# From the MLP to the attention: context turned among the last down products, norm sums by panels, the first key products in two halves

## The chip, the core and the metric

The kernel runs on one core of a Trainium2 chip. Its time is the device time of one execution in microseconds (us); three executions of the kernel before took 2696.97, 2700.23 and 2701.65 us, median 2700.23. One more execution was profiled. TensorE (PE) multiplies, VectorE (DVE), ScalarE (ACT) and GpSimd (POOL) do the rest, and SyncE (SP) issues the loads of the weights.

## The reference, cut to what matters

Two transformer blocks run one after the other on 256 tokens of width 2048, all in float32. The place in question is the end of the first block and the start of the second.

```python
x = x + squared_relu_mlp(h, w_mlp_in[l], w_mlp_out[l])      # end of the first block
x = rmsnorm(x, norm_final)
# the second block
sh1, sc1, g1, sh2, sc2, g2 = split(silu(c) @ w_ada + b_ada)  # csh1, csc1 the same from c_ctx
h  = modulate(rms_norm(x, norm_mix_g), sh1, sc1)             # y * (1 + scale) + shift
hc = modulate(rms_norm(ctx, norm_mix_g), csh1, csc1)
y  = neighbourhood_attention(h, hc, w_qkv, ...)              # keys and values of h and hc, queries of h
x  = x + g1 * y
```

Each norm divides a row by the root of its mean square plus 1e-6. So x is normed twice in a row: by `norm_final`, and again for the attention.

## The kernel before, in words

Every product in full precision is three float32r products of split operands: a weight unit (128 rows, 1024 numbers of each) comes by DMA into one of four slots of `raw`, ScalarE copies its rounded part to `whi`, VectorE subtracts to get `wlo` (`split`, lines 611 and 975), and TensorE multiplies hi by hi, hi by lo and lo by hi. The activations stand transposed in `act2` (`ahi`, `alo`), per 128 features k a slot of 512 numbers: 256 tokens in the left half, 256 in the right. The semaphores `hi_done`, `lo_done` and `unit_used` order the units; a slot can be filled again when TensorE has used the unit four before.

The MLP has four groups. In a group 32 up units fill `G[q]` in PSUM and ScalarE and VectorE write the squared ReLU into the right halves of `act2`; then 32 down units (`unit_rows`, line 1554) make four panels of 512 columns in turn in `G[0]` and `G[1]`, and VectorE adds each to x (`add_scaled`, line 1234). Beside that VectorE sums the modulation's columns from `w_ada`, which GpSimd loads (line 510).

After the last panel, in program order: VectorE and ScalarE square one row tile of x each (lines 979 and 615, 2048 numbers a partition), ScalarE forms the root (617, 618), VectorE multiplies by it and by `norm_final` (1301), both square again (`ROW_NORMS` numbers these norms), and both scale into `xs` (984, 827). Meanwhile ScalarE squares and scales the context `ctxr` (822, 829). TensorE then transposes `xs` in eight steps of four 128 by 128 blocks each, and likewise `ctxr` (`turn_rows`, line 1599, turns 3 and 4). For each step ScalarE writes the rounded, modulated value (630), VectorE the unrounded one (997), GpSimd subtracts them into `alo` (540), and TensorE's buffers in PSUM, `X[0]` to `X[3]`, come free with that. x stands in the left halves of `act2`, the context in the right.

The attention has eight turns (`na_turn`) of twelve units: m = 0 to 3 keys for x and context at once (512 tokens wide, line 1911), 4 to 7 queries (1916), 8 to 11 values (1922). The first turn also multiplies a diagonal of the gate g1 by ones to spread it over the partitions (`spread_early`; 1324 builds it, 1929 and 1933 multiply), and each turn sums 32 terms of the later modulation (`ada_tail`, lines 1242 and 1243, 384 wide), whose eight loads GpSimd issues into two buffers (552). A load waits until the one two before it is used up. TensorE adds the sums over the partitions after m = 9 and m = 11 (`ada_sums`, 1808).

The order of work on each engine is the order of the code; nothing reorders it. In the tables of rows, `ps` is PSUM, `act` is `act2`, `arena` the shared scratch area that also holds `xs`, `ctxr`, `nfin` and the loads of `w_ada`.

Of the kernel before, what the change touches and what calls it, by code (L numbers as in the profile page):

```python
# [19 lines left out]
F32 = mybir.dt.float32  # L20
F32R = mybir.dt.float32r
ACT = mybir.ActivationFunctionType
ALU = mybir.AluOpType
# [3 lines left out]
P = 128  # L27
# [94 lines left out]
ROW_NORMS = (0, 2, 3, 4)  # L122
# [36 lines left out]
def program(nc, t, out):  # L159
    ctx = ExitStack()  # L160
    with ctx:
# [13 lines left out]
        ahi, alo = act2[:, 0], act2[:, 1]  # L175
        x = sb("x", [P, RT, D])
# [73 lines left out]
        turned_f = area(8448, 2, 2, S)  # L250
# [11 lines left out]
        psq, rms2 = sb("psq", [P, RT, 4]), sb("rms2", [P, RT])  # L262
        acc3 = sb("acc3", [P, TAIL_W])
# [46 lines left out]
        psq_ok = sem("psq_ok")  # L310
        hid_a, hid_v = sem("hid_a"), sem("hid_v")
# [58 lines left out]
        def _(sp):  # L370
# [94 lines left out]
            for n in range(4):  # L465
                sp.wait_ge(x_done, 4 + n)
# [6 lines left out]
        def _(pool):  # L473
# [55 lines left out]
            for e in range(4, 8):  # L529
                ada_load(ADA_N - 1, e)  # L530
# [12 lines left out]
            turn(3, 0)  # L543
            turn(4, S)

            pool.wait_ge(turned, 8 * 5)
# [19 lines left out]
        def _(act):  # L566
# [232 lines left out]
            with own.loop(0, 4, 4) as g:  # L799
                with own.loop(0, 2, 2) as i:  # L800
                    for j in range(4, 20):
                        split(g * 64 + i * 16 + U_MLP, j)
                        if j % 8 == 3:
# [7 lines left out]
                                           sqr.rearrange("p (c t) -> p c t", t=S), ACT.Copy).then_inc(hid_a, 1)  # L811
                with act.Fori(0, 2) as i:
                    for j in range(4, 20):
                        split(g * 64 + i * 16 + (U_MLP + 32), j)


            act.wait_ge(x_done, 1)
            rms_rows(2, x[:, 0, :], xs[:, 0, :])
            act.wait_ge(ctx_in, 16)
            act.wait_ge(ada_col, ADA_N)  # L820
            for r in range(RT):
                own.done(act.activation(area(4096, D), ctxr[:, r, :], ACT.Square, accum_out=ssum[:, 10 + r:11 + r]))
            own.done(act.activation(rstd[:, 10:12], ssum[:, 10:12], ACT.Ln, scale=1.0 / D, bias=EPS))
            act.activation(rstd[:, 10:12], rstd[:, 10:12], ACT.Exp, scale=-0.5).then_inc(ctx_rs, 1)
            act.wait_ge(x_done, 2)
            rms_rows(3, x[:, 0, :], xs[:, 0, :])
            act.activation(xs[:, 0, :], x[:, 0, :], ACT.Copy, scale=rstd[:, 6:7]).then_inc(xs_ok, 1)
            act.wait_ge(ctx_rs, 1)
            act.activation(ctxr[:, 0, :], ctxr[:, 0, :], ACT.Copy, scale=rstd[:, 10:11]).then_inc(ctx_ok, 1)
            act.wait_ge(coef_ok, 2)  # L830
            turn(3, 0, lambda k: coefs[:, k:k + 1], lambda k: mods[:, k:k + 1])
            turn(4, S, lambda k: coefs[:, 16 + k:17 + k], lambda k: modc[:, k:k + 1])
# [23 lines left out]
            def na_turn(i, first):  # L856
                u0 = i * 12 + U_NA
                for m in range(12):
# [10 lines left out]
                    if m == 6:  # L869
                        inv_rms(i, 0)  # L870
# [25 lines left out]
            act.wait_ge(x_done, 3)  # L896
# [63 lines left out]
        def _(dve):  # L960
# [268 lines left out]
            def add_scaled(n, q, used, done):  # L1229
# [6 lines left out]
                ins.then_inc(done, 1)  # L1236
# [26 lines left out]
            def mlp_half(g, up, cx):  # L1263
# [756 lines left out]
```

## Time and profile before

| | us |
|---|---|
| median of three runs | 2700.23 |
| the profiled execution | 2695.33 |
| its span, first to last instruction | 2693.1 |
| TensorE busy | 2569.5 |
| VectorE, ScalarE, GpSimd busy | 1743.4, 1152.9, 183.2 |

The profile is of one execution of 2695.33 us; the 2.2 us beside its span lie around the first and last instruction. Busy shares are over the whole span. A matmul's busy time overlaps its successor's, so a unit's length is read from the starts or from the merged pieces of the chain of waits, not from the mean of one. The granted clock is a share of 2.4 GHz: 0.5 is the level of 1.2 GHz. Times of single rows count from the span's start.

### The profile page before, as it was taken

What the parts mean: (1) busy time and instruction counts of PE and PEld (TensorE: products, weight loads), DVE (VectorE), ACT (ScalarE), POOL (GpSimd) and SP (SyncE); (2) the same over time, 40 slices, a digit from 0 to 9 for tenths busy, and PEclk for the clock granted to TensorE, in tenths of its full rate; (3) what the DMA queues carried; (4) which work ended last, traced back from release to release, by engine and by line L of the source; (5) the groups of instructions that cost most, each with busy time, mean ns of one, the idle gap of its engine ahead of it and who ended that gap; (6) DMA issues with size and microseconds to landing.
All of it is one profiled execution on the core that took longest, in us unless ns stands there. A gap on an engine that the chain in (4) does not pass through costs nothing.

```text
span 2693.1 us, 42214 instructions
## 1 busy us (share of the span) xinstructions
PE 2569.5 (95%) x15397; PEld 2272.8 (84%) x15397; DVE 1743.4 (65%) x2194; ACT 1152.9 (43%) x1421; POOL 183.2 (7%) x213
## 2 busy tenths in 40 slices
PE   4999988999999999996999999998889999999999
PEld 4989877998988989985888888886678888888887
DVE  4555455778877876667666666665556665666576
ACT  3444344543443543445233333333455534554453
POOL 2100004000000000003000000000010000000000
PEclk8999999999999999997999999998989999999999
DMA  6743369778777877772666665652546656656555
GB/s 159 247 124 98 117 192 265 267 233 275 237 247 244 259 240 248 251 238 90 194 194 193 193 186 181 191 174 82 184 125 187 187 191 183 187 187 202 179 181 173
DMA packets 277976, 523.87 MB, mean 195 GB/s; under 512 B 30697, under 2 KB 100897, under 8 KB 277089
## 3 DMA queue, kind: packets, MB, share of 16 engines
q1 hardware_dynamic: 251616, 403.66, 47.3%
q0 software_dynamic: 25536, 118.29, 14.6%
q8 instruction: 81, 1.33, 0.2%
q10 hardware_dynamic: 704, 0.29, 0.0%
q14 instruction: 39, 0.31, 0.0%
HBM read 511.68 MB, written 10.49 MB: 194 GB/s over the span
## 4 chain that ended last, share of the span: by engine, by line
PE 47%; DVE 3%; ACT 1%; issue 1%; POOL 1%; DMA 0%; ACTq 0%; POOLq 0%; DVEq 0%; SPq 0%
PE ps L1554 12%; PE ps L1573 11%; PE ps L1911 6%; PE ps L1576 6%; PE ps L1922 5%; PE ps L1916 3%; PE ps L1879 1%; PE ps L1858 1%; POOL act L540 1%; PE ps L1887 1%; DVE acc L1243 1%; PE ps L1867 1%; ACT whi L611 0%; DVE wlo L975 0%; PE ps L1808 0%
## 5 line engine op out<-in xcount | busy, mean ns | idle before, releaser
L975 DVE TENSOR_TENSOR wlo<-raw,whi 128x1024 fp32r<-128x1024 f32 (+2 forms) x776 | 939.1, 1218 | 589.6 <-ACT whi L611 569.5
L611 ACT ACTIVATE whi<-raw 128x1024 fp32r<-128x1024 f32 (+2 forms) x776 | 803.3, 1040 | 993.4 <-PE ps L1554 407.7
L1554 PE MATMUL ps<-whi,act 128*128 128x512 f32 (+2 forms) x2608 | 794.2, 386 | 18.4 <-DVE wlo L975 16.2
L1554 PEld LDWEIGHTS ps<-whi,act 128*128 128x128 f32 x2608 | 485.9, 190 | 113.0 <-DVE wlo L975 15.1
L1546 PE MATMUL ps<-act,whi 128*128 128x256 f32 (+2 forms) x2880 | 529.9, 286 | 12.9 <-DVE wlo L975 10.8
L1554 PE MATMUL ps<-wlo,act 128*128 128x512 f32 (+2 forms) x1304 | 501.0, 384 | 0.0
L1546 PEld LDWEIGHTS ps<-act,whi 128*128 128x128 f32 (+1 forms) x2880 | 453.2, 192 | 15.0 <-issue 11.3
L1546 PE MATMUL ps<-act,wlo 128*128 128x256 f32 (+2 forms) x1440 | 410.6, 285 | 0.0
L1573 PE MATMUL ps<-act,whi 128*128 128x512 f32 x1376 | 378.4, 396 | 5.9 <-POOL act L540 4.6
L1554 PEld LDWEIGHTS ps<-wlo,act 128*128 128x128 f32 x1304 | 247.1, 190 | 45.8
L1243 DVE SCALAR_TENSOR_TENSOR arena<-arena,cond 128x768 f32<-128x768 f32 (+1 forms) x330 | 278.7, 867 | 4.6 <-DMA arena<-in_w_ada 1.8
L1546 PEld LDWEIGHTS ps<-act,wlo 128*128 128x128 f32 (+1 forms) x1440 | 276.5, 192 | 1.3 <-issue 1.3
L1573 PEld LDWEIGHTS ps<-act,whi 128*128 128x128 f32 x1376 | 235.5, 189 | 37.8 <-issue 5.0
L1576 PEld LDWEIGHTS ps<-act,wlo 128*128 128x128 f32 x1376 | 212.6, 189 | 30.1
L1576 PE MATMUL ps<-act,wlo 128*128 128x256 f32 x1376 | 220.7, 281 | 0.0
L1922 PE MATMUL ps<-whi,act 128*128 128x256 f32 x1024 | 192.1, 290 | 0.0
L1922 PEld LDWEIGHTS ps<-whi,act 128*128 128x128 f32 x1024 | 160.4, 192 | 7.7 <-issue 7.7
L1911 PE MATMUL ps<-act,whi 128*128 128x512 f32 x512 | 164.4, 402 | 0.0
L1922 PE MATMUL ps<-wlo,act 128*128 128x256 f32 x512 | 144.8, 283 | 0.0
L1911 PEld LDWEIGHTS ps<-act,whi 128*128 128x128 f32 x512 | 95.4, 190 | 22.0 <-issue 3.9
L1911 PE MATMUL ps<-act,wlo 128*128 128x512 f32 x256 | 100.6, 393 | 0.0
L1916 PE MATMUL ps<-act,whi 128*128 128x256 f32 x512 | 98.4, 293 | 0.0
(254 smaller groups left out, 1938.6 us busy)
## 6 DMA issues: line engine op xcount, KB each, us to landing
arena<-in_w_ada POOLq DMA_DIRECT2D x128, 768.0 KB, 5.6
raw<-in_ffn_w_up SPq DMA_DIRECT2D x160, 512.0 KB, 4.4
raw<-in_w_mlp_in SPq DMA_DIRECT2D x128, 512.0 KB, 5.1
raw<-in_w_mlp_out SPq DMA_DIRECT2D x128, 512.0 KB, 4.8
raw<-in_na_w_qkv SPq DMA_DIRECT2D x96, 512.0 KB, 4.7
raw<-in_ffn_w_down SPq DMA_DIRECT2D x84, 512.0 KB, 4.5
raw<-in_w_in SPq DMA_DIRECT2D x64, 384.0 KB, 3.4
raw<-in_w_in SPq DMA_DIRECT2D x32, 512.0 KB, 4.6
```

Source lines behind the costliest of these rows:

```text
L540: pool.tensor_tensor(alo[:, k, off:off + S], turned_f[:, at % 2], ahi[:, k, off:off + S].bitcast(F32), ALU.subtract).then_inc(a_lo, 2)
L611: act.activation(a, b, ACT.Copy).then_inc(hi_done, 1)
L975: dve.tensor_tensor(a, b, c, ALU.subtract).then_inc(lo_done, 1)
L1243: return dve.scalar_tensor_tensor(out=acc, in0=piece, scalar=sc, in1=acc, op0=ALU.mult, op1=ALU.add)
L1546: ins = pe.matmul(o, a, b, start=start and i == 0, stop=last and i == 2, skip_group_check=True)
L1554: ins = pe.matmul(o, a, b, start=start and i == 0, stop=last and i == 2, skip_group_check=True)
L1573: pe.matmul(Z[q][:, c, :].rearrange("p (h t) -> p h t", h=2), kn(whi, j)[:, kk, P * c:P * c + P], act2[:, :, k, 0:S], start=k == 0, stop=k ...
L1576: ins = pe.matmul(Z[q][:, c, 0:S], kn(wlo, j)[:, kk, P * c:P * c + P], ahi[:, k, 0:S], start=False, stop=k == KC - 1, skip_group_check=True)
L1858: pe.matmul(X[1], qT[:, hh, P * qb:P * qb + P], kT[:, hh, :], start=True, stop=True).then_inc(n_s, 1)
L1911: ins = pe.matmul(G[0][:, c, :], a, b, start=st and y == 0, stop=sp_ and y == 2)
L1916: ins = pe.matmul(X[0][:, S * c:S * c + S], a, b, start=st and y == 0 and c == 0, stop=sp_ and y == 2, skip_group_check=True)
L1922: ins = pe.matmul(Gf[1][:, S * r:S * r + S], a, b, start=st and y == 0 and r % 2 == 0, stop=sp_ and y == 2, skip_group_check=True)
```

## The change

The rows of the context are squared, scaled, transposed and modulated before and during the last group: its squares and its root stand between the third group and the fourth; its eight turn steps stand behind every second down unit of the last group's first two panels (`ctx_step`). The two norms of x are formed together: for each panel of 512 columns, as soon as it is complete, ScalarE squares x and x times `norm_final` (`final_squares`, `final_product`), so that after the last panel one panel's squares are left; the scale for `xs` comes from both sums at once, and x itself gets its first norm later (`residual_rows`, in the first turn's m = 0). x now stands in the right halves of `act2`, where the hidden values were, and the context in the left half of the next slot. The first turn's keys are made for the context first and for x after (`first_keys`), x's turn steps between. In the other seven turns the last of the sixteen k of the key units is multiplied as two pieces of 256 instead of one of 512. The gate's spreading moves behind m = 4 and 6, the first turn's `ada_tail` slots to m = 5 to 11.

```diff
+FIRST_TAIL = {5: (0,), 6: (1,), 7: (2,), 8: (3, 4, 5), 9: (6, 7, 8), 10: (9, 10), 11: (11,)}
-ROW_NORMS = (0, 2, 3, 4)
+ROW_NORMS = (0, 4)
...
+        def own_rows(h, c, t0, n):
+            return act2[:, h, c, S + t0:S + t0 + n]
+        def ctx_rows(h, c, t0, n):
+            at = (512 * c + 512) % (512 * KC)
+            return both[:, h, at + t0:at + t0 + n]
...
+            for e, steps in ((4, (0, 1)), (5, (2, 3)), (6, (4, 5)), (7, (6, 7))):
+                ada_load(ADA_N - 1, e)
+                for at in steps:
+                    turn_lo(3, at)
+            for at in range(8):
+                turn_lo(4, at)
-            pool.wait_ge(turned, 8 * 5)
+            pool.wait_ge(x2_ok, 1)
...
+            mlp_up(3)
+            def final_squares(n):
+                act.wait_ge(drained[n % 2], D_MLP[n % 2] - 1 + n // 2)
+                for r in range(RT):
+                    own.done(act.activation(junk_a, x[:, r, cs], ACT.Square, accum_out=fsq[:, r, n:n + 1]))
+                act.wait_ge(y_ok, n + 1)
+                for r in range(RT):
+                    own.done(act.activation(junk_a, xs[:, r, cs], ACT.Square, accum_out=fsq[:, 2 + r, n:n + 1]))
...
+            for j in range(4, 35):
+                split(U_MLP + 3 * 64 + 32, j)
+                if j % 2 == 1 and j < 20:
+                    turn_step(3, (j - 5) // 2)
+                if j % 8 == 5 and j > 8:
+                    final_squares(j // 8 - 1)
...
+            act.wait_ge(fvar_ok, 1)
+            own.done(act.activation(frms[:, 1, :], frms[:, 0, :], ACT.Ln))
+            act.activation(frms[:, 1, :], frms[:, 1, :], ACT.Exp, scale=-0.5).then_inc(frms_ok, 1)
+            act.wait_ge(frms_ok, 1)
+            scale_piece(0, xs, xs, frms[:, 1, 0:1])
+            scale_piece(1, xs, xs, frms[:, 1, 0:1])
+            split(U_NA, 3)
+            turn_step(4, 0)
...
+            own.done(dve.tensor_reduce(fsum[:, :], fsq[:, :, :], AXX, ALU.add))
+            own.done(dve.tensor_scalar(frms[:, 0, :], fsum[:, 0:2], EPS / D, EPS * EPS, ALU.mult, ALU.add))
+            dve.scalar_tensor_tensor(out=frms[:, 0, :], in0=fsum[:, 2:4], scalar=1.0 / D, in1=frms[:, 0, :],
+                                     op0=ALU.mult, op1=ALU.add).then_inc(fvar_ok, 1)
...
+            def residual_rows():
+                dve.wait_ge(r1_ok, 1)
+                for r in range(RT):
+                    own.mark(dve.scalar_tensor_tensor(out=x[:, r, :], in0=x[:, r, :], scalar=frms[:, 2, r:r + 1], in1=nfin,
+                                                      op0=ALU.mult, op1=ALU.mult))
+                own.wait()
+                dve.sem_inc(x2_ok, 1)
...
+            def ctx_step(at):
+                if at >= 2:
+                    pe.wait_ge(a_lo, TURN_AT[3] + 2 * at - 2)
...
+                            if last and i == 0 and j % 2 == 1:
+                                ctx_step(4 * q + j // 2)
...
+            def own_steps(steps):
+                for at in steps:
+                    pe.wait_ge(xs_a, at // 2 + 1)
+                    pe.wait_ge(xs_v, at // 2 + 1)
...
+            def first_keys():
+                pe.wait_ge(a_lo, TURN_AT[4])
+                for m in range(4):
+                    pe.wait_ge(lo_done, U_NA + m + 1)
+                    half_keys(m, *w(m), ctx_rows, S, True)
+                    if m:
+                        own_steps(range(2 * m - 2, 2 * m))
+                for m in range(4):
+                    pe.wait_ge(a_lo, TURN_AT[4] + 4 * m + 4)
+                    half_keys(m, *w(m), own_rows, 0, False).then_inc(unit_used, 1)
+                    if m == 0:
+                        own_steps(range(6, 8))
...
-                    if first and m == 0:
+                    if first and m == 4:
                         pe.wait_ge(gb_ok, 1)
```

TensorE from the last down product to the first key products. Before, 16 steps of four transposes stand in one piece between the down products (line 1554) and the keys (1911).

```order
L1554 MATMUL ps<-whi,act2 128x512 x2
L1554 MATMUL ps<-wlo,act2 128x512
L1841 REGISTER_ALU
L1841 COMPARE_AND_BRANCH
L1599 MATMUL ps<-cst,arena 128x128 x64
L1911 MATMUL ps<-act2,whi 128x512 x2
L1911 MATMUL ps<-act2,wlo 128x512
```

After, the context's transposes (line 1996 of the changed kernel) stand among the down products (1726), four at a time.

```order
L1726 MATMUL ps<-whi,act2 128x512 x2
L1726 MATMUL ps<-wlo,act2 128x512
L1996 MATMUL ps<-cst,arena 128x128 x4
L1726 MATMUL ps<-whi,act2 128x512 x2
L1726 MATMUL ps<-wlo,act2 128x512
```

And x's (2046) stand, eight at a time, between half-wide key products (2056).

```order
L2056 MATMUL ps<-act2,whi 128x256 x2
L2056 MATMUL ps<-act2,wlo 128x256
L2046 MATMUL ps<-cst,arena 128x128 x8
L2056 MATMUL ps<-act2,whi 128x256 x2
L2056 MATMUL ps<-act2,wlo 128x256
```

The 64 transposes are divided into twelve pieces, eight in the down products and four in the keys, and the keys are twice as many and half as wide.

VectorE from the last panel's addition (1234 before, 1332 after) to the gate's diagonal (1324 before, 1492 after). Before:

```order
L1234 SCALAR_TENSOR_TENSOR x<-ps,rms,x 128x512 x2
L1284 COPY mods<-ps 128x6
L151 REGISTER_ALU
L151 COMPARE_AND_BRANCH
L979 ISA arena,stat<-x 128x2048
L979 ISA stat 128x1
L1301 SCALAR_TENSOR_TENSOR x<-x,stat,arena 128x2048 x2
L979 ISA arena,stat<-x 128x2048
```

After, from the root's last term to the diagonal (1463 scales `xs`, 1425 is the turn step, 1481 the residual's norm, 1073 a split):

```order
L1457 SCALAR_TENSOR_TENSOR frms<-fsum,frms 128x2
L1463 TENSOR_SCALAR arena<-arena,frms 128x512 x2
L1073 TENSOR_TENSOR wlo<-raw,whi 128x1024
L1425 TENSOR_SCALAR arena<-ps,coefs,mods 128x256 x2
L1463 TENSOR_SCALAR arena<-arena,frms 128x512
L1425 TENSOR_SCALAR arena<-ps,coefs,mods 128x256 x2
L1463 TENSOR_SCALAR arena<-arena,frms 128x512
L1425 TENSOR_SCALAR arena<-ps,coefs,mods 128x256 x12
L1481 SCALAR_TENSOR_TENSOR x<-x,frms,arena 128x2048 x2
L1073 TENSOR_TENSOR wlo<-raw,whi 128x1024
L1490 TENSOR_TENSOR mods<-mods,cols 128x16
L1492 TENSOR_SCALAR arena<-cst,mods 128x128 x16
```

The long product with `norm_final` has moved from ahead of the transposes to behind them, and it stands ahead of the split of the first query unit and of the diagonal.

VectorE at the end of the first turn (m = 9 to 11). Before:

```order
L1243 SCALAR_TENSOR_TENSOR acc<-arena,cond,acc 128x384 x4
L975 TENSOR_TENSOR wlo<-raw,whi 128x1024
L1243 SCALAR_TENSOR_TENSOR acc<-arena,cond,acc 128x384 x4
L1368 SCALAR_TENSOR_TENSOR arena<-ps,cols,arena 128x512
L1388 COPY mods<-ps 128x3
L975 TENSOR_TENSOR wlo<-raw,whi 128x1024
L1243 SCALAR_TENSOR_TENSOR acc<-arena,cond,acc 128x384 x4
```

After:

```order
L1347 SCALAR_TENSOR_TENSOR arena<-arena,cond 128x384 x2
L1346 TENSOR_SCALAR acc<-arena,cond 128x384
L1347 SCALAR_TENSOR_TENSOR acc<-arena,cond,acc 128x384 x3
L1073 TENSOR_TENSOR wlo<-raw,whi 128x1024
L1347 SCALAR_TENSOR_TENSOR acc<-arena,cond,acc 128x384 x8
L1536 SCALAR_TENSOR_TENSOR arena<-ps,cols,arena 128x512
L1556 COPY mods<-ps 128x3
L1073 TENSOR_TENSOR wlo<-raw,whi 128x1024
L1347 SCALAR_TENSOR_TENSOR acc<-arena,cond,acc 128x384 x4
```

Six terms stand at m = 9 now and eight at m = 10, where four and four stood; none is left at m = 0 to 4.

## Rows read from the trace of the kernel before

**Rows 1.** The page of before: busy time of the two busiest engines.
```profile
PE 2569.5 (95%) x15397; PEld 2272.8 (84%) x15397; DVE 1743.4 (65%) x2194; ACT 1152.9 (43%) x1421; POOL 183.2 (7%) x213
```

**Rows 2.** Stretches after the down products: length; busy PE, PEld, DVE, ACT, POOL; clock; DMA; GB/s.
```profile
1230.20:1266.60 36.40, 16.61 (x64) 11.84 (x64) 28.28 (x44) 28.80 (x47) 15.76 (x13) 0.53 0.08 26
1266.60:1277.10 10.50, 10.11 (x33) 6.98 (x33) 6.95 (x21) 2.31 (x4) 5.84 (x6) 0.85 0.36 107
1277.10:1293.40 16.30, 16.30 (x74) 13.48 (x74) 10.63 (x15) 2.12 (x2) 2.51 (x4) 1.00 0.74 238
1293.40:1333.10 39.70, 39.39 (x310) 37.26 (x309) 25.84 (x34) 14.24 (x18) 3.49 (x6) 1.00 0.67 209
1333.10:1402.70 69.60, 69.30 (x460) 61.74 (x460) 45.29 (x75) 23.14 (x35) 6.55 (x10) 1.00 0.61 188
```

**Rows 3.** Timeline of TensorE around the seam: start, length, work, idle before.
```profile
1229.77 0.39 PE L1554 MATMUL ps<-wlo,act 128*128 128x512 f32 x1
1246.61 3.67 PE L1599 MATMUL ps<-cst,arena 128*128 128x128 f32 x16 [16.45 <-ACT arena L827]
1251.95 2.35 PE L1599 MATMUL ps<-cst,arena 128*128 128x128 f32 x8 [1.67 <-POOL act L540]
...
1266.67 1.20 PE L1911 MATMUL ps<-act,whi 128*128 128x512 f32 x2
```

**Rows 4.** Timeline of VectorE in the same stretch.
```profile
1232.43 1.40 DVE L1234 SCALAR_TENSOR_TENSOR x<-ps,rms,x 128x512 f32<-128x512 f32 x2
...
1236.88 4.61 DVE L1301 SCALAR_TENSOR_TENSOR x<-x,stat,arena 128x2048 f32<-128x2048 f32 x2 [0.57 <-ACT stat L618]
...
1249.46 1.90 DVE L997 TENSOR_SCALAR arena<-ps,coefs,mods 128x256 f32<-128x256 f32 x4 [2.43 <-ACT act L630]
...
1269.42 4.70 DVE L1324 TENSOR_SCALAR arena<-cst,mods 128x128 f32<-128x128 f32 x16
...
1287.96 0.62 DVE L1243 SCALAR_TENSOR_TENSOR arena<-arena,cond 128x384 f32<-128x384 f32 x1 [1.76 <-DMA arena<-in_w_ada]
```

**Rows 5.** Timeline of ScalarE, same stretch.
```profile
1236.41 0.20 ACT L617 ACTIVATE stat<-stat 128x2 f32<-128x2 f32 x1 [0.50 <-DVE stat L979]
...
1248.35 3.73 ACT L630 ACTIVATE act<-ps,mods,coefs 128x256 fp32r<-128x256 f32 x8
```

**Rows 6.** Timeline of GpSimd, same stretch.
```profile
1250.64 20.32 POOL L540 TENSOR_TENSOR act<-arena,act 128x512 fp32r<-128x512 f32 x16 [69.06 <-DVE arena L997]
...
1281.46 0.75 POOL L552 DMA_DIRECT2D arena<-in_w_ada  x1 [8.04 <-DVE arena L1243]
```

**Rows 7.** Chain of waits, in order of time: attention units at full clock.
```profile
1277.07 16.33 PE ps L1911 x72
...
1300.02 2.87 PE ps L1916 x24
...
1319.54 5.85 PE ps L1922 x48
```

**Rows 8.** TensorE earlier: transposes at full clock.
```profile
428.54 1.04 PE L1599 MATMUL ps<-cst,x 128*128 128x128 f32 x8
```

**Rows 9.** ScalarE earlier: one square of 512 with its sum.
```profile
478.00 0.63 ACT L786 ACTIVATE arena<-x 128x512 f32<-128x512 f32 x1
478.54 0.19 ACT L786 ACTIVATION_READ_ACCUMULATOR arena<-x 128x1 f32 x1
```

**Rows 10.** VectorE at the boundary of turns 0 and 1.
```profile
1329.67 2.57 DVE L1243 SCALAR_TENSOR_TENSOR acc<-arena,cond,acc 128x384 f32<-128x384 f32 x4
1333.31 0.16 DVE L1388 COPY mods<-ps 128x3 f32 x1 [1.06 <-PE ps L1808]
```

**Rows 11.** Loads of the modulation's columns (line 552).
```profile
DMA to landing us min/median/max: 4.9/5.3/7.5
```

**Rows 12.** VectorE's splits with and without GpSimd beside them.
```profile
442.58 7.75 DVE L975 TENSOR_TENSOR wlo<-raw,whi 128x1024 fp32r<-128x1024 f32 x4
...
459.61 1.23 DVE L975 TENSOR_TENSOR wlo<-raw,whi 128x1024 fp32r<-128x1024 f32 x1 [1.19 <-ACT whi L611]
```

More of the change, by code:

```diff
@@ L798, in _, with mlp_up @@
             act.sem_inc(psq_ok, 1)
-            with own.loop(0, 4, 4) as g:
+            def mlp_up(g):
                 with own.loop(0, 2, 2) as i:
@@ L814, in _ @@
                         split(g * 64 + i * 16 + (U_MLP + 32), j)
-            act.wait_ge(x_done, 1)
-            rms_rows(2, x[:, 0, :], xs[:, 0, :])
             act.wait_ge(ctx_in, 16)
-            act.wait_ge(ada_col, ADA_N)
             for r in range(RT):
-                own.done(act.activation(area(4096, D), ctxr[:, r, :], ACT.Square, accum_out=ssum[:, 10 + r:11 + r]))
+                for half in range(2):
+                    own.done(act.activation(area(3072, 1024), ctxr[:, r, 1024 * half:1024 * half + 1024], ACT.Square,
+                                            accum_out=fsq[:, r, half:half + 1]))
@@ L835, in attend_a @@
+            for at in range(3, 8):
+                turn_step(4, at)
             def attend_a(i, m):
@@ L869, in na_turn @@
                     if m == 6:
+                        if first:
+                            act.wait_ge(x2_ok, 1)
                         inv_rms(i, 0)
@@ L1267, in mlp_half @@
                     for j in range(4, 20):
-                        split(u0, j)
+                        end = last and i == 1 and j == 19
+                        if not end:
+                            split(u0, j)
                         slot = 16 * i + j - 4
@@ L1317, in _ @@
-            turn(3, 0, lambda k: coefs[:, k:k + 1], lambda k: mods[:, k:k + 1])
-            turn(4, S, lambda k: coefs[:, 16 + k:17 + k], lambda k: modc[:, k:k + 1])
+            dve.wait_ge(nf_in, 16)
+            mlp_half(3, False, False, True)
+            cs3 = slice(1536, D)
+            for r in range(RT):
+                ins = dve.tensor_tensor(xs[:, r, cs3], x[:, r, cs3], nfin[:, cs3], ALU.mult)
+                if r == 0:
+                    ins.then_inc(y_ok, 1)
+                else:
+                    own.done(ins)
@@ L1890, in na_turn @@
                 u0 = i * 12 + U_NA
-                for m in range(12):
+                if first:
+                    first_keys()
+                for m in range(4 if first else 0, 12):
                     part = m // 4
@@ L1930, in na_turn @@
                         ins.then_inc(gb_mm, 1)
-                    if first and m == 5:
+                    if first and m == 6:
                         pe.wait_ge(gb_rd, 1)
```

230 lines of the change are left out of this document (176 added, 54 removed).

## The prediction

> **What bounds the kernel now.** First the page: TensorE is busy for 2569.5 of 2693.1 us [rows 1], so a change pays only where TensorE stands or runs slowly. Then the busy times by stretch [rows 2]: the reader is to see that the 36.4 us after the last down product hold only 16.6 us of TensorE at 0.53 of its clock, and that the next stretches are full at 1.00. Then TensorE's timeline [rows 3]: the last down product ends at 1230.2 (E below), 16.45 us are empty, and from 1246.6 on 64 transposes run in bursts that GpSimd releases, until the first key product at 1266.7. The timelines of the other three say why. Ahead of the transposes stands a chain on VectorE and ScalarE in which every link handles 2048 columns, the longest 4.61 us [rows 4]. In the transposes GpSimd works without a break, 20.32 us for 16 steps, 1.27 each [rows 6]. The first group of keys then waits once more, for the gate's diagonal, which ends at 1274.1 [rows 4].
>
> I measure from E to the start of turn 1 at 1333.1: 102.9 us before. Behind it the eight turns are periodic, 69.6 us at 69.3 busy [rows 2], and the change touches them in one place only.
>
> **What the change costs outside the seam.** Eight context steps of four transposes go into the last down units. Eight transposes at full clock took 1.04 us, start to end [rows 8], some 0.13 each with the overlap off; 0.55 a step, 4.4 us in all, wholly on TensorE's path. The bounds are 0.5 and 1.27 a step (GpSimd's pace, if a buffer is not free), 4 to 10; I take 4.4, since a buffer has two steps, some 12 us, to come free. A down unit is twelve 512-wide products. 72 of them in the keys took 16.33 us [rows 7], so 0.227 each and 2.72 a unit. In two units and a step, 6.0 us, VectorE has two splits (1.23 each [rows 12]), one 768-wide term (at most two of the 384-wide at 0.62 [rows 4], 1.24) and a turn step (0.95 [rows 4]), 4.65 in sum; ScalarE two copies of about 1.1, a step of 0.94 [rows 5] and, at three places, four squares of 0.73 [rows 9]. Both fit, and the splits run three units ahead, which covers the 2.6 us of addition and product at a panel's end. So nothing more falls on the path. The context's squares, root and scaling on ScalarE at the start of the fourth group take four squares of 1024 (an estimate from the 512-wide at 0.73: 1.2), two small operations of 0.2 with hand-overs (0.8) and one copy of 2048 (four of 512-wide at 0.5: 2.0), about 7.6 us with the split's 1.1 ahead 8.7, against four up units (2.88 each, as 24 products of 256 took 2.87 [rows 7]): just covered with a split and its subtraction behind it, 0 to 2 us, I take 0. The last k of the keys as 256-wide pieces costs 12 times 0.12 instead of 6 times 0.227 in each of seven turns, 0.5 us together.
>
> **The seam after, from E.** VectorE adds the last panel by rows, 1.4 us [rows 4]; ScalarE squares behind it. VectorE forms the last product and a square over 512 columns, 1.25 and 0.7; three small operations 0.9, two on ScalarE 0.5 [rows 5], one scaled piece 0.6. Sum with hand-overs: xs's first piece stands at E+5.5. TensorE meanwhile does the context half: 96 products of 256, 2.88 a unit. It wants its first x step after two of them, at E+5.8. This margin of 0.3 is thin, and the last links are estimates from rows of other widths; bounds for the wait are 0 and 3, I take 0. The x steps then run on ScalarE in E+7 to E+20.3 (each 0.94 to 1.02, with a split of 1.06, two scalings and the second root between), one behind on VectorE until E+21.3, and on GpSimd until E+22.6. TensorE needs them only unit by unit in the second half; its own work is 8 times 2.88 plus 32 transposes at 0.137, so the keys end at E+27.4 against E+63.2 before.
>
> From there VectorE sets the pace. Behind its last turn step at E+21.3 stand in order: the two long products, 4.6 [rows 4]; a split, 1.2; the gate's diagonal, 0.2 and 4.6 [rows 4]. That is E+32.1. The query unit ends at E+30.3, so TensorE waits 1.8 us and its three gate products end at E+34.7. VectorE goes on with four splits, 4.6, and the gate's copy, 1.7, and starts its 32 terms only at E+38.4, where before nine were already done when the keys ended. A load takes, from the term that frees its buffer to its use, 6.5 us: 1281.46 [rows 6] to 1287.96 [rows 4]; from issue to landing 4.9 to 7.5, median 5.3 [rows 11]. Walking through m = 5 to 11 with terms at 0.62, splits at 1.2 and norms at 0.75: the third load is wanted at E+47.0 and there at E+48.4; the fifth at E+57.2, there at E+60.0; the seventh at E+66.2, there at E+68.9. The last four terms, 2.57 as at 1329.67 [rows 10], end at E+75.9. TensorE's own work from the keys' end (the wait of 1.8, the gate 3.4, four units of 2.87, four of 5.75 [rows 7], the norm and column sums 3.2) ends at E+70.3, so it stands for 5.6 us before the last column sums. Turn 1 starts at E+76.8, 26.1 earlier than before. Before, it waited there too, but for a fraction: 1329.67 plus 2.57 is 1332.2, and turn 1's first work follows at 1333.1. After so long a stand the first products run at 1.2 GHz; at 1266.7 that stretch of 10.5 us showed 0.85 of the clock [rows 2], a loss of 1.5, and I take 1.3.
>
> Sum: -26.1 + 4.4 + 0.5 + 1.3 = -19.9 us. The profiled execution, 2695.3, becomes 2675.4. It lay 4.9 below the median of the three runs, so against this median I predict 2680.3.
>
> **A rule that speaks against it.** With GpSimd's work beside them, four splits of VectorE took 7.75 us, 1.94 each; without it one took 1.23 [rows 12]. In the change GpSimd's last two x steps fall beside the two long products at E+21.3. By a delay of this size they end some 1.4 us later, and the keys about as much; VectorE's list behind it shifts by 0.7 at most, and the time with it. The Trainium skill (SBUF — State Buffer, engine ports and the shared port pair) says that VectorE's instructions with two SBUF inputs and GpSimd's exclude one another for the whole instruction. By that rule, an estimate, GpSimd could stand for both long products, the last keys would end 2.7 us later, and about 1 us of it would reach turn 1. The trace agrees that the two slow each other, and cannot show the order of the two here.
>
> **The rivals.**
> Dense end: the terms are not late, because loads land sooner or VectorE's list is shorter than I count. For it: TensorE alone is done at E+70.3, and in the turns of before loads stopped VectorE for 1.76 us once [rows 4]. Against: VectorE begins the terms some 10 us after the keys. The stand of 5.6 and the clock's 1.3 fall away: -26.8, 2673.4.
>
> Broken first keys: the norm's root comes late and TensorE stands inside the keys, so that its clock falls while narrow products and short transposes alternate. For it: margin 0.3, and in bursts of transposes the clock stayed at 0.5 for 20 us [rows 2, 3]. Against: products stand between, and at 428.5 transposes among products went at full pace [rows 8]. If half the keys run at 1.2 GHz, they take 12 to 14 more, of which the stand of 5.6 absorbs a part: -10 to -14, about 2688. If all do, 25 more: -1, 2699, no change.
>
> Slower: the last group's down products lose the pace. VectorE's turn step waits for ScalarE's, ScalarE's for the transposes, and GpSimd's subtraction, now beside splits and terms with two SBUF inputs, adds 0.7 to each of three operations in a pair of units [rows 12]: 4.65 becomes 6.75 against 6.0. That alone costs 6 over eight pairs. It decides once short stands pull the clock down: at 1.2 GHz the 16 units take 43 more, of which 14 more suffice to undo the gain: 6 + 43 - 20 is 29 slower at the full price, 2729. The splits' three units in hand speak against.
>
> **How the numbers follow.** Forecast 0.47; dense end 0.20; broken keys in part 0.22, in full 0.03; slower 0.05; 0.03 for a gain beyond the dense end. For the forecast alone the range is 2675 to 2686 (VectorE's list by 3 us either way, runs by 2). The whole range takes in the dense end and the broken keys in part: 2668 to 2692. What a measurement tells from no change is about 0.2%, 5.4 us, so faster has the forecast, the dense end and all partial cases: 0.92; same 0.03; slower 0.05.
>
> **What would show it.** In the profile after: the context transposes among down units that otherwise keep 2.72; the first x transposes some 6 us after the last down product, TensorE above 95% busy at clock 1.00 until the gate; keys done near E+27; a wait of about 2 us for the gate's diagonal; loads of `w_ada` as releasers of VectorE at m = 7, 9 and 10; a wait of 5 to 6 us before line 1808's successor, released by VectorE's terms; turn 1 at E+77. It is wrong if the clock falls inside the keys, if the down units of the last group lengthen, or if turn 1 starts before E+72 or after E+82.

## The result, and the profile after

| | before | after |
|---|---|---|
| median of five runs, us | 2698.93 | 2686.70 |
| lowest and highest | 2696.54 to 2701.65 | 2682.38 to 2691.88 |
| profiled execution, and its span | 2695.33, 2693.1 | 2682.38, 2680.7 |

The ratio of the times is 0.995, 95% interval 0.9934 to 0.9966: 13.5 us faster, between 9.2 and 17.8 (the medians themselves differ by 12.2). Predicted were 2680.3, a range of 2668 to 2692, and 19.9 us of gain. So the sign and the whole range held; the gain came out smaller, and the forecast's own narrower range, 2675 to 2686, was missed by 0.7.

The page of the changed kernel: TensorE is busy for as long as before [rows 1], in a shorter span.

```profile
PE 2569.4 (96%) x15535; PEld 2281.1 (85%) x15535; DVE 1747.9 (65%) x2205; ACT 1159.0 (43%) x1454; POOL 197.9 (7%) x221
```

Busy times by stretch, columns as in [rows 2]. E, the end of the last down product, is now 1239.5.

```profile
1239.50:1266.90 27.40, 26.68 (x224) 26.30 (x222) 21.24 (x33) 17.05 (x34) 12.45 (x8) 1.00 0.11 37
1266.90:1280.00 13.10, 12.18 (x82) 10.15 (x81) 12.36 (x27) 4.09 (x4) 1.51 (x2) 1.00 0.83 277
1280.00:1298.50 18.50, 17.43 (x133) 16.03 (x131) 14.21 (x20) 6.96 (x9) 3.02 (x5) 1.00 0.87 275
1298.50:1317.30 18.80, 13.96 (x106) 13.28 (x105) 12.70 (x20) 4.15 (x5) 3.52 (x5) 0.92 0.72 235
1317.30:1387.90 70.60, 70.36 (x459) 62.55 (x458) 45.21 (x75) 21.30 (x32) 5.79 (x8) 0.97 0.59 185
```

Where 36.4 us held 16.6 of TensorE at a clock of 0.53, 27.4 us now hold 26.7 at 1.00: the keys are done in them as well. The last two lines carry what spoils it: the end of turn 0 is short of work (13.96 of 18.80), and turn 1 runs at 0.97 and takes 70.6 where it took 69.6.

TensorE's timeline, from the first context step on (columns as in [rows 3]; products left out). Lines of the changed kernel: 1996 context steps, 2046 x steps, 2056 first keys, 2152 queries, 2166 gate, 1980 column sums.

```profile
1152.49 0.66 PE L1996 MATMUL ps<-cst,arena 128*128 128x128 f32 x4 [1.50 <-DVE arena L1441]
...
1158.49 0.60 PE L1996 MATMUL ps<-cst,arena 128*128 128x128 f32 x4
...
1245.23 1.06 PE L2046 MATMUL ps<-cst,arena 128*128 128x128 f32 x8
...
1249.01 1.04 PE L2046 MATMUL ps<-cst,arena 128*128 128x128 f32 x8
...
1264.00 0.50 PE L2056 MATMUL ps<-act,whi 128*128 128x256 f32 x2 [0.69 <-POOL act L569]
...
1267.62 0.47 PE L2152 MATMUL ps<-act,whi 128*128 128x256 f32 x2 [0.48 <-DVE wlo L1073]
...
1271.16 2.84 PE L2166 MATMUL ps<-arena,cst 128*128 128x512 f32 x6 [0.44 <-DVEq L1494]
...
1297.78 0.80 PE L1980 MATMUL ps<-cst,arena 128*128 128x1 f32 x6 [1.07 <-DVE arena L1347]
...
1315.88 1.44 PE L1980 MATMUL ps<-cst,acc 128*128 128x1 f32 x6 [4.84 <-DVE acc L1347]
1317.18 1.20 PE L2147 MATMUL ps<-act,whi 128*128 128x512 f32 x2
```

These are all waits above 0.3 us between the first context step and turn 1. The 16.45 us of [rows 3] and GpSimd's bursts are gone; what stands instead is 4.84 us before the last column sums, released by VectorE's terms, and the two products behind it take 1.20 us where at full clock they take 0.62 to 0.71. The busy times there, the clock at its lower level of 1.2 GHz:

```profile
1316.00:1321.00 5.00, 5.00 (x15) 4.23 (x16) 1.35 (x2) 0.00 (x0) 0.75 (x1) 0.50 0.95 293
```

VectorE in the same stretch (1481 products for x, 1492 the gate's diagonal, 1346 and 1347 the terms):

```profile
1244.33 0.88 DVE L1463 TENSOR_SCALAR arena<-arena,frms 128x512 f32<-128x512 f32 x2 [0.58 <-ACT frms L915]
...
1260.03 6.07 DVE L1481 SCALAR_TENSOR_TENSOR x<-x,frms,arena 128x2048 f32<-128x2048 f32 x2
...
1267.59 3.45 DVE L1492 TENSOR_SCALAR arena<-cst,mods 128x128 f32<-128x128 f32 x16
...
1277.41 0.41 DVE L1346 TENSOR_SCALAR arena<-arena,cond 128x384 f32<-128x384 f32 x1
...
1287.97 0.62 DVE L1347 SCALAR_TENSOR_TENSOR arena<-arena,cond 128x384 f32<-128x384 f32 x1 [1.75 <-DMA arena<-in_w_ada]
...
1300.44 0.42 DVE L1346 TENSOR_SCALAR acc<-arena,cond 128x384 f32<-128x384 f32 x1 [2.81 <-DMA arena<-in_w_ada]
...
1308.77 2.58 DVE L1347 SCALAR_TENSOR_TENSOR acc<-arena,cond,acc 128x384 f32<-128x384 f32 x4 [2.19 <-DMA arena<-in_w_ada]
...
1313.25 2.57 DVE L1347 SCALAR_TENSOR_TENSOR acc<-arena,cond,acc 128x384 f32<-128x384 f32 x4
```

The first term starts 10 us after the keys are done, loads are then waited for, and the last four terms end at 1315.8, where TensorE had run out of work at 1311.0.

Four rows of column sums mark the program in every version: A, at the end of the last group's up half; B, 4.3 us before E; C, at the end of turn 0; D, at the end of the last turn. All the versions run below, with the differences between the starts of these rows, from one profile each, in us. Each ratio is to executions of before taken beside that version (medians 2698.9 to 2700.9):

| kernel | median, us | ratio to before | A to B | B to C | C to D |
|---|---|---|---|---|---|
| before | 2698.93 | 1 | 88.56 | 106.38 | 487.37 |
| after | 2686.70 | 0.9950 (0.9934 to 0.9966) | 94.04 | 80.67 | 490.22 |
| tail_early | 2676.40 | 0.9921 (0.9906 to 0.9935) | 94.03 | 75.39 | 487.81 |
| terms_cut | 2674.32 | 0.9914 (0.9896 to 0.9932) | 94.03 | 75.58 | 487.79 |
| steps_first | 2693.77 | 0.9976 (0.9967 to 0.9986) | 94.03 | 90.64 | 490.27 |
| squares_late | 2689.64 | 0.9958 (0.9944 to 0.9972) | 94.05 | 88.21 | 490.08 |
| ctx_late | 2708.13 | 1.0027 (1.0016 to 1.0038) | 88.56 | 109.77 | 489.89 |
| both_mended | 2673.68 | 0.9897 (0.9883 to 0.9911) | 92.31 | 75.69 | 487.84 |
| rows_wait | 2675.26 | 0.9899 (0.9869 to 0.9929) | 92.31 | 76.02 | 487.82 |

From before to after the three stretches give +5.5, -25.7 and +2.9, together -17.4. The two spans differ by 12.4. The missing 5.0 lie where both kernels run the same instructions: 0.9 up to the first group's column sums at 577, 2.9 from there to the end of the third group, 1.2 behind the last turn. Where the times of two versions are compared below, the difference of their ratios is taken, times 2700.

### The profile page after: what moved, and what is told of

It is laid out like the page before. It is cut to its first block, busy times and chain, and to the rows that moved or that the text cites. A ratio compares the mean times of both kernels' runs of the same rounds, so it can differ in the third digit from the quotient of the medians.

```text
span 2680.7 us, 42529 instructions
## 1 busy us (share of the span) xinstructions
PE 2569.4 (96%) x15535; PEld 2281.1 (85%) x15535; DVE 1747.9 (65%) x2205; ACT 1159.0 (43%) x1454; POOL 197.9 (7%) x221
## 4 chain that ended last, share of the span: by engine, by line
PE 86%; DVE 6%; DMA 3%; ACT 2%; issue 1%; SPq 1%; ACTq 0%; POOL 0%; POOLq 0%; DVEq 0%
PE ps L1726 30%; PE ps L1718 18%; PE ps L1745 12%; PE ps L1748 6%; PE ps L2147 5%; PE ps L2159 5%; PE ps L2152 3%; DMA raw<-in_w_in 1%; PE ps L2106 1%; SPq L434 1%; PE ps L2085 1%; DVE wlo L1073 1%; DVE acc L1347 1%; PE ps L1980 1%; PE ps L2114 1%
## 5 line engine op out<-in xcount | busy, mean ns | idle before, releaser
L1745 PE MATMUL ps<-act,whi 128*128 128x512 f32 x1376 | 379.3, 396 | 6.3 <-POOL act L555 4.9
L1726 PEld LDWEIGHTS ps<-wlo,act 128*128 128x128 f32 x1304 | 247.5, 190 | 45.7
L1745 PEld LDWEIGHTS ps<-act,whi 128*128 128x128 f32 x1376 | 236.1, 190 | 38.4 <-issue 5.3
L2147 PE MATMUL ps<-act,whi 128*128 128x512 f32 x420 | 135.7, 405 | 0.0
L935 ACT ACTIVATE arena<-arena,nst 128x512 f32<-128x512 f32 x32 | 23.2, 724 | 175.2 <-DVE nst L1520 175.2
L2159 PEld LDWEIGHTS ps<-wlo,act 128*128 128x128 f32 x512 | 98.0, 191 | 0.0
```

The source lines that it names most:

```text
L1726: ins = pe.matmul(o, a, b, start=start and i == 0, stop=last and i == 2, skip_group_check=True)
L1745: pe.matmul(Z[q][:, c, :].rearrange("p (h t) -> p h t", h=2), kn(whi, j)[:, kk, P * c:P * c + P], act2[:, :, k, 0:S], start=k == 0, stop=k ...
L2147: ins = pe.matmul(G[0][:, c, :], a, b, start=st and y == 0, stop=False, skip_group_check=True)
L2159: ins = pe.matmul(Gf[1][:, S * r:S * r + S], a, b, start=st and y == 0 and r % 2 == 0, stop=sp_ and y == 2, skip_group_check=True)
```

## The experiments

**Are VectorE's late terms what stops TensorE? (tail_early)** The terms of the first turn are handed out by loads instead of by slots, as many as have landed: eight already at m = 5, and the second sum from m = 9.

```diff
-FIRST_TAIL = {5: (0,), 6: (1,), 7: (2,), 8: (3, 4, 5), 9: (6, 7, 8), 10: (9, 10), 11: (11,)}
+FIRST_TAIL = {5: (0, 8), 7: (8, 12), 8: (12, 16), 9: (16, 24), 10: (24, 28), 11: (28, 32)}
...
-                        for slot in FIRST_TAIL.get(m, ()):
-                            ada_tail(i, slot)
+                        if m in FIRST_TAIL:
+                            ada_tail(i, None, range(*FIRST_TAIL[m]))
```

> The changed kernel with the 32 terms of the first turn's modulation dealt out otherwise: eight at m = 5, none at 6, four at 7 and 8, eight at 9, four at 10 and 11, so that both buffers are free for the next loads by about 1282.5 on the changed kernel's time axis (1286.2 there). Theory A (the stand before turn 1 is the alternation of loads and terms on VectorE): the last term ends at about 1311 instead of 1315.8, TensorE's two waits for terms (4.8 and 1.1 us) shrink to 1 or less and turn 1 starts at full clock; 6 to 8 us faster than the changed kernel's 2686.7, so about 2679. Rival B (the loads themselves cannot come sooner, since weights share the queues): within 2 us of 2686.7.

TensorE's timeline at the end of turn 0, and the busy times from there to the end of turn 1:

```profile
1311.64 0.83 PE L1980 MATMUL ps<-cst,acc 128*128 128x1 f32 x6 [0.85 <-DVE acc L1347]
```

```profile
1298.00:1311.60 13.60, 12.79 (x102) 12.11 (x101) 11.34 (x18) 3.82 (x5) 2.25 (x3) 1.00 0.86 271
1311.60:1381.30 69.70, 69.36 (x464) 62.02 (x464) 45.23 (x75) 22.64 (x34) 6.56 (x9) 1.00 0.62 195
```

The wait falls from 4.84 to 0.85 and the one of 1.07 goes; B to C is 5.3 shorter, C to D 2.4, together 7.7; the ratios differ by 7.8 us, as expected. So the stand cost its own length and 2.4 of clock behind it, where I had put 1.3.

**The same with the terms taken away (terms_cut).** Twenty-two of the first turn's 32 terms are left out, so that part of the modulation isn't summed.

```diff
+                    if cut and k and k % 4 != 3:
+                        continue
                     ins = ada_term(s, k, ada2[:, q % 2, k % 4, :], (acc2, acc3[:, :])[s], 0, k == 0)
```

> The changed kernel without 22 of the 32 terms of the first turn's modulation (only the first of each sum and the last of each load are left); the loads all stay. Theory A: VectorE is free for the loads' pace, TensorE does not stand before turn 1: 6 to 8 us faster than 2686.7. Rival B (only the loads' pace counts): the last load lands as late as before, gain 0 to 2 us. Rival C (the time of the changed kernel is lost outside the seam, in the clock's dips during the MLP): the stand goes away in the trace, and the median moves by less than its spread of 5 us.

```profile
1313.20 0.83 PE L1982 MATMUL ps<-cst,acc 128*128 128x1 f32 x6 [1.05 <-DVE acc L1347]
```

VectorE's last term there:

```profile
1312.53 0.62 DVE L1347 SCALAR_TENSOR_TENSOR acc<-arena,cond,acc 128x384 f32<-128x384 f32 x1 [1.94 <-DMA arena<-in_w_ada]
```

It is 9.7 us faster than after, a little more than the 6 to 8 expected; the rival that the time was lost outside the seam is out. With a third of the work B to C is 75.6, no less than in tail_early. The 1 us that is left waits for the last load here. In tail_early no load is waited for at that place: the last four terms follow a split at once, from 1309.0 to 1311.6. So either way of removing the lateness leaves TensorE about 1 us.

**Is it the interleaving that keeps the clock up? (steps_first)** All x steps stand ahead of the keys.

```diff
                 pe.wait_ge(a_lo, TURN_AT[4])
+                own_steps(range(8))
                 for m in range(4):
                     pe.wait_ge(lo_done, U_NA + m + 1)
                     half_keys(m, *w(m), ctx_rows, S, True)
-                    if m:
-                        own_steps(range(2 * m - 2, 2 * m))
```

> The changed kernel with all eight x turn steps ahead of the first key products, context half then x half unbroken. Theory A (VectorE's list sets the start of turn 1, and TensorE has slack of 6 us in the first turn): the keys end some 11 us later (about E+39), the steps 3 to 5 us sooner, and the whole is 3 to 6 us slower than 2686.7, with the clock's fall in it. Rival D (the gain lies in the context products under x's norm): 11 to 14 us slower, which gives back the whole gain.

TensorE's timeline, and the busy times from E on:

```profile
1246.04 3.65 PE L2046 MATMUL ps<-cst,arena 128*128 128x128 f32 x16 [5.77 <-DVE arena L1463]
1251.09 0.66 PE L2046 MATMUL ps<-cst,arena 128*128 128x128 f32 x4 [1.40 <-POOL act L569]
1252.50 0.65 PE L2046 MATMUL ps<-cst,arena 128*128 128x128 f32 x4 [0.75 <-POOL act L569]
1253.82 2.34 PE L2046 MATMUL ps<-cst,arena 128*128 128x128 f32 x8 [0.67 <-POOL act L569]
```

```profile
1239.00:1266.60 27.60, 18.90 (x112) 17.12 (x111) 20.43 (x32) 13.87 (x31) 12.35 (x8) 0.75 0.14 42
```

TensorE stands for 8.6 us and the stretch runs at 0.75 of the clock instead of 1.00. The keys end at E+40.6. B to C grows by 10.0, the time by 7.0: more than the 3 to 6 that I expected, less than the rival's 11 to 14. The terms' stand shrinks to 3.71, so only a part of the loss is absorbed there. The interleaving of context keys and x steps is thus worth 7 to 10 us of the gain.

**Are the squares by panels worth anything? (squares_late)** All squares of ScalarE wait until its last weight split.

```diff
-                if j % 8 == 5 and j > 8:
-                    final_squares(j // 8 - 1)
+            for n in range(3):
+                final_squares(n)
             cs3 = slice(1536, D)
```

> The changed kernel with the squares of the first three panels (twelve squares of 512 on ScalarE) behind the last split instead of among the down units. Theory A: the norm's root comes 12 x 0.76 = 9.1 us later less what ScalarE finds free before the last panel (about 2), so xs's first piece is at E+11 to 13 instead of E+5.8, TensorE stands 5 to 7 us inside the first keys, and everything behind on VectorE moves with it: 7 to 11 us slower than 2686.7, with the clock's fall. Rival D: the norm sums are hidden either way, 0 to 2.

```profile
1257.96 1.94 PE L2046 MATMUL ps<-cst,arena 128*128 128x128 f32 x8 [4.71 <-DVE arena L1463]
```

TensorE now waits for the scale of `xs`, 4.71 us, and the transposes behind it take 1.94 where they took 1.06: half clock. B to C grows by 7.5, as theory A has it. The time grows only by 2.2, where 7 to 11 were expected, and the two intervals overlap. The profiled execution is the slowest of the ten (2698.1, median 2689.6), and the granted clock over the whole execution was 0.981 in five of them (2683.0 to 2690.5 us) but 0.976 to 0.978 in the other five, this one included (2685.8 to 2698.1). The profile shows the mechanism in one execution; whether every execution pays for it, and what it costs in time, is not settled by these runs.

**The context's steps behind the last down product (ctx_late).** The steps are moved whole: TensorE's, ScalarE's, VectorE's and GpSimd's, which issues its four loads ahead of them. Besides, the context's unrounded values go to another place in the scratch area, and so do the square's discarded values on VectorE, and VectorE's third product no longer waits for GpSimd's steps.

```diff
-                            if last and i == 0 and j % 2 == 1:
-                                ctx_step(4 * q + j // 2)
...
             mlp_turn(3, None, last=True)
+            for at in range(8):
+                ctx_step(at)
```

> The changed kernel with the context's eight turn steps behind the last down product (on ScalarE and VectorE behind the first two scaled pieces of x) instead of among the down units. Theory A: the down units lose 5.5 us (eight steps of 0.5 and the wait of 1.5), but the steps take 8 x 1.27 at GpSimd's pace from E+6 on, and the context's keys and all of VectorE's list come behind them: turn 1 starts 10 to 12 us later after E; net 5 to 8 us slower than 2686.7, with a fall of the clock in the stand before. Rival D (the steps were not worth moving, since they cost TensorE full time among the down units): 0 to 3 us slower or faster.

TensorE's and GpSimd's timelines (1994 the context steps there, 565 the subtractions for them):

```profile
1249.56 1.11 PE L1994 MATMUL ps<-cst,arena 128*128 128x128 f32 x4 [9.92 <-POOL act L565]
1250.92 1.12 PE L1994 MATMUL ps<-cst,arena 128*128 128x128 f32 x4 [0.25 <-POOL act L565]
1254.36 1.12 PE L1994 MATMUL ps<-cst,arena 128*128 128x128 f32 x4 [2.33 <-POOL act L565]
1255.73 1.12 PE L1994 MATMUL ps<-cst,arena 128*128 128x128 f32 x4 [0.26 <-POOL act L565]
```

```profile
1252.90 2.77 POOL L565 TENSOR_TENSOR act<-arena,act 128x256 fp32r<-128x256 f32 x4 [2.04 <-DVE arena L1418]
1257.71 2.78 POOL L565 TENSOR_TENSOR act<-arena,act 128x256 fp32r<-128x256 f32 x4 [2.03 <-DVE arena L1418]
```

```profile
1250.00:1270.00 20.00, 10.85 (x45) 8.48 (x44) 5.97 (x12) 6.12 (x12) 9.21 (x14) 0.50 0.01 3
```

It is slower than before by 7.3 us (4.3 to 10.3), and 21 slower than after, where I expected 5 to 8. I had counted GpSimd's pace, 1.27 a step. The rows show another limit: with two buffers a pair of steps comes round every 4.8 us (1249.56, 1254.36, and 1252.90 to 1257.71), GpSimd stands for 2.04 of it, and TensorE's clock is at 0.50 throughout. In [rows 6], with four buffers, GpSimd never stood. A to B is 88.56, the value of before, so the steps alone make the 5.5 us of the down half; and having them there saves far more than it costs.

**The best of both (both_mended).** The wait of 1.50 before the first context step is VectorE's scaling of the context's second row tile (line 1441), which stands in its program behind the last group's whole up half. Here tail_early is kept and the scaling stands ahead of that half.

```diff
+            dve.wait_ge(ctx_rs, 3)
+            dve.tensor_scalar(ctxr[:, 1, :], ctxr[:, 1, :], rstd[:, 11:12], None, ALU.mult).then_inc(ctx_ok, 1)
             mlp_half(3, True, False)
-            dve.wait_ge(ctx_rs, 3)
-            dve.tensor_scalar(ctxr[:, 1, :], ctxr[:, 1, :], rstd[:, 11:12], None, ALU.mult).then_inc(ctx_ok, 1)
```

> tail_early, and besides the scaling of the context's second row tile on VectorE moved from behind the fourth group's up half to ahead of it, where VectorE stands 3.5 us for ScalarE. Theory A: the wait of 1.5 us ahead of the first context step, which every trace of the changed kernel has, goes away and nothing takes its place; 1 to 2 us faster than tail_early's 2676.4, 10 to 13 faster than the changed kernel. Rival: the wait is replaced by one for the first up units of the group, no gain over tail_early.

TensorE's timeline at the first context step, no wait ahead of it:

```profile
1148.97 0.60 PE L1996 MATMUL ps<-cst,arena 128*128 128x128 f32 x4
```

A to B is 92.31 instead of 94.03, 1.7 less. At 2673.68 this has the lowest median: a ratio of 0.9897 to before, 27.8 us, twice the change's own gain. Against tail_early I expected 1 to 2 us. The ratios differ by 6.5, but their intervals overlap; the trace shows 1.7 of it.

**Do the long products and GpSimd exclude each other? (rows_wait)** both_mended, but VectorE starts its two products for x only when GpSimd has done its last subtraction.

```diff
                 dve.wait_ge(r1_ok, 1)
+                dve.wait_ge(a_lo, OT_AT)
                 for r in range(RT):
```

> both_mended with one wait more: VectorE's two long products for the residual wait until GpSimd's last x step is done. Theory G (the two engines exclude each other: each product of 2048 columns holds GpSimd's next piece back and the other way round): GpSimd's last two pieces take 2.5 us together instead of 4.6, the two products 4.6 instead of 6.1; TensorE's wait of 0.70 us in the keys goes, the products end within 0.6 us of before, and the time stays within 1 us. Rival H (the products are slow by themselves, through their scalar's source): the products still take 6.1, all behind moves by 2.4 us and the time by 1 to 2.5.

VectorE's, GpSimd's and TensorE's timelines:

```profile
1264.29 4.61 DVE L1482 SCALAR_TENSOR_TENSOR x<-x,frms,arena 128x2048 f32<-128x2048 f32 x2 [1.91 <-POOL act L569]
```

```profile
1261.64 2.54 POOL L569 TENSOR_TENSOR act<-arena,act 128x512 fp32r<-128x512 f32 x2 [1.22 <-DVE arena L1425]
```

```profile
1270.43 0.47 PE L2153 MATMUL ps<-act,whi 128*128 128x256 f32 x2 [1.98 <-DVE wlo L1073]
```

Apart from one another the two take 4.61 and 2.54; together, in after, 6.07 and 4.57, and the same in both_mended. So the products aren't slow by themselves (rival H). The wait for GpSimd (0.69) goes, one of 1.98 for VectorE's split comes, B to C is 0.3 longer, and the time is the same within its interval.

**Both kernels unchanged, once more each (before_again, after_again).**

> The kernel before, unchanged, for a second trace. Theory E (how often the clock falls near the column sums of the first three groups, untouched by the change, is chance): the spans from the first column sums (576.5) to those at the end of the third group (1041.1, so 464.6 in the first trace) comes out anywhere from 464 to 468. Rival F (the changed kernel is slower there for a reason in its code): again 464.6, within 0.5.

> The changed kernel, unchanged, for a second trace. Theory E: the same span, 467.5 in its first trace, varies by 1.5 us or more. Rival F: again 467.5 within 0.5. Both expect the last down product to turn 1's column sums at 76.4 within 0.5, since no load and no clock decides there.

They took 2698.30 and 2686.81. A to B, B to C and C to D came again: 88.55, 106.45 and 487.43 for before, 94.03, 80.85 and 490.55 for after, so -17.0 us in place of -17.4. The last down product to turn 1's column sums took 76.6, within the 0.5 expected, though loads have a part in it: VectorE's terms wait for them.

The stretch from the first group's column sums to the end of the third group, the same instructions in all versions, took 464.6 us in the profile of before, 467.5 in that of after, but 467.6 and 467.7 in the repeats, and 465.0 in those of tail_early and both_mended. The repeat of after alone came as rival F has it; the repeat of before, and the two versions with after's code there, rule F out. So the 2.9 us between the first two profiles are not the change's. Busy times of before and of after where such a loss lies, the first row a part of the second:

```profile
952.40:955.80 3.40, 3.40 (x18) 3.40 (x18) 0.00 (x0) 0.00 (x0) 0.00 (x0) 0.51 0.65 227
952.00:977.00 25.00, 25.00 (x118) 21.51 (x118) 15.96 (x19) 11.39 (x11) 0.71 (x1) 0.93 0.56 186
```

```profile
652.00:677.00 25.00, 25.00 (x121) 21.16 (x121) 15.60 (x16) 8.41 (x8) 1.43 (x2) 0.93 0.76 247
```

TensorE is busy all the time, and the clock falls to its lower level of 1.2 GHz for a few microseconds. Such a fall follows some of the short bursts of column sums, one burst in each half of a group, 2 to 4 us behind the burst's start. Of the six bursts from 577 to 1050 it followed three in before (falls at 580, 952 and 1044), all six in after, and four in each repeat. From the first burst to the second every profile took 91.4 us with one fall and 89.9 without, so one costs 1.5. Up to the end of the third group after has five of them and before two, so three more, 4.6 us by this price. A shorter wait of TensorE near 860, 0.51 us in after where before has 0.89 and 1.17, gives 1.5 of it back, which leaves about the 2.9. Why one burst is followed by a fall and the next isn't stays open.

## Why the prediction was right, and where it was off

**The seam.** Predicted from E: first x transposes at +5.8, measured +5.7; keys done +27.4, measured +27.7; gate's products start at +32.1 after a wait of 1.8, measured +31.7 after 0.44, with 0.69 and 0.48 of short waits ahead that I hadn't; first term +38.4, measured +37.9; last term ends +75.9, measured +76.3; turn 1's first key product +76.8, measured +77.7, against 102.9 before. So -25.2 where I had -26.1. 0.6 of the 0.9 between the two are the column sums ahead of turn 1, which ran at half clock: from their start to turn 1's first key product it is 1.30, in terms_cut 0.69. The margin before the first x transposes is as thin as it was counted, 0.3: TensorE starts on them at 1245.23, the first scaled piece was done at 1244.8 on VectorE and at 1245.0 on ScalarE. The profile of squares_late shows the price of missing it.

**Two errors in VectorE's list that cancel.** The two products for x took 6.07, not 4.6; the gate's diagonal 3.45, not 4.6. That 1.5 too little and 1.2 too much cancel is luck. Both come from GpSimd. One line of each kernel, for its single instructions (minimum, median, maximum in ns; first and last start):

```profile
L1324 DVE TENSOR_SCALAR arena<-cst,mods x16: 268/278/1336, 1269.4 to 1273.8; 128x128 f32<-128x128 f32 x16
```

```profile
L1492 DVE TENSOR_SCALAR arena<-cst,mods x16: 269/282/595, 1267.6 to 1270.8; 128x128 f32<-128x128 f32 x16
L1481 DVE SCALAR_TENSOR_TENSOR x<-x,frms,arena x2: 2783/3072/3361, 1260.0 to 1262.7; 128x2048 f32<-128x2048 f32 x2
L569 POOL TENSOR_TENSOR act<-arena,act x4: 1288/1291/3321, 1255.6 to 1260.6; 128x512 fp32r<-128x512 f32 x4
```

Of before's sixteen pieces of the diagonal one, the second, took 1336 ns: it ended at 1271.05, just behind GpSimd's last subtraction, which ends at 1270.96 [rows 6]. The 4.6 that I carried over from [rows 4] contained this wait. That GpSimd caused it is read from these times and from its absence in after; no run tests it. For the products, in after, the order is plain: the first product ended at 1262.82; GpSimd's last subtraction, begun at 1260.63, ended at 1263.95, 1.1 behind it; the second product, begun at 1262.74, ended at 1266.10, 2.2 behind that. Alone they take 1.3 and 2.3. So that subtraction took 3321 ns instead of 1290, and each product was held back by one subtraction at most. In the prediction such a delay put the end of the last keys 1.4 us later by [rows 12], 2.7 by the page's rule with GpSimd standing for both products. GpSimd stood for one; of its 2.0 us 0.69 reached TensorE, and the keys ended 0.3 behind the forecast. The Trainium skill (SBUF — State Buffer, who interferes with whom) says that a VectorE instruction with two inputs in SBUF contends with a GpSimd instruction that reads SBUF, and that whoever issues first holds the shared ports for the whole instruction. The trace agrees, and rows_wait shows both durations without the other.

**The stand and the clock.** Predicted 5.6 for the wait and 1.3 for the clock; measured 4.84 and 1.07 in two places, 5.9 together, and 2.4. The clock's term was mis-sized: I took it from a stretch of 10.5 us at 0.85 [rows 2], but here the column sums ahead of turn 1 and its first products ran at half clock, 0.50 from 1316 to 1321. tail_early and terms_cut remove both at once and bring turn 1 back to 69.7 us.

**The down half.** Predicted 4.4, measured 5.5. The eight steps cost 0.47 each, their spacing of 5.9 less two units of 2.72, and 3.75 in all (A to B of both_mended less before's), where I took 0.55. The rest, 1.7, is the wait of 1.50 and what hangs on it, for VectorE's scaling of the context. I had priced the context's norm at 0 to 2 on ScalarE, took 0, and never asked for the half of it that stands on VectorE behind 32 splits. That is the step that failed: of a moved chain I followed one engine only. both_mended shows 1.7 us for it.

**The turns.** The last k in two pieces: predicted 0.5, measured 0.4 to 0.5 (C to D 487.8 in the versions without the stand, 487.4 before).

**The sum.** The traced terms give -17.4 where I had -19.9; 1.1 of the difference is the down half, 0.9 the seam, the rest, 0.5, the clock behind turn 1's start. The measured gain is 13.5, with 17.4 still inside its interval (9.2 to 17.8). Between the two lie stretches that the change doesn't touch; in the repeats these differ by up to 3 us from one execution to the next, through falls of the clock. Whether all of these 4 us are chance is not shown: over the other versions the traced gain exceeds the measured one by up to 3.8 (tail_early) and falls short by up to 1.3 (both_mended, squares_late).

**The rivals.** Dense end: it didn't come, but tail_early is that case made on purpose, 7.7 us better in the trace where the rival was priced 6.9 better. Broken keys in part: by the number alone, 13.5, it would fit this rival's price of 10 to 14, but the clock stayed at 1.00 in the keys; steps_first and squares_late show what it costs when the pace breaks, 10.0 and 7.5 in the profile, where the rival was priced 6 to 10 worse than the forecast. Down products losing pace: no wait above 0.3 in them but the first.

## What to carry to other kernels

When work is pulled forward out of a gap, price what stood in the gap's shadow: here VectorE's list, whole before the keys ended, became the last to end, and reordering it was worth 7.8 us beside the change's own 13.5. Follow a moved chain on every engine that has a link in it, and look for the program position behind which each link stands. A duration taken from a trace may contain a block by another engine: look at the minimum and maximum of the single instructions before it becomes a term.

## What the runs showed of the hardware

- Four bursts of eight transposes, one every 3.8 us among products of 256 columns, left TensorE's clock at 1.00 over the 27.4 us of the first keys (after). Transposes alone, behind a wait of 9.9 us and with waits of up to 2.3 between them, had 0.50 in the same place (ctx_late).
- Behind a wait of 4.84 us TensorE's clock was at 0.50, and this cost 2.4 us; behind waits of 0.85 and 1.05 at the same place this loss was absent (tail_early, terms_cut).
- VectorE's instructions with two inputs in SBUF and GpSimd's subtractions ran one after the other, instruction by instruction: 6.07 and 4.57 together, 4.61 and 2.54 apart.
- A turn of two PSUM buffers over ScalarE, VectorE and GpSimd back to TensorE, one step in each, took 4.8 us, at 1.39 per step for the slowest of the three (2.77 for four subtractions, two steps).
- A busy TensorE had falls to half clock behind some bursts of one-column products, more or fewer from one execution to the next, 1.5 us for each. The runs of one kernel spread over 5 to 15 us of 2700.
